# A two-layer diffusion backbone on one core: the start of the first layer reordered around its ada tiles

## The reference

```python
mod_x = (jax.nn.silu(c) @ w_ada[i] + b_ada[i])[:, None, :]
mod_c = (jax.nn.silu(c_ctx) @ w_ada[i] + b_ada[i])[None, None, :]
sh1, sc1, gt1, sh2, sc2, gt2 = jnp.split(mod_x, 6, axis=-1)
csh1, csc1, cgt1, csh2, csc2, cgt2 = jnp.split(mod_c, 6, axis=-1)
hx = rmsnorm(x, g_pre1[i]) * (1.0 + sc1) + sh1
hc = rmsnorm(e, g_pre1[i]) * (1.0 + csc1) + csh1
ux = hx @ w_in[i]
```

## Time and profile before

| | us |
|---|---|
| median of 3 runs (lowest, highest) | 2218.12 (2217.26, 2218.92) |
| time of the profiled execution | 2219.41 |
| span of the profiled execution | 2217.6 |
| TensorE busy in it | 2129.1 (96%) |
| VectorE, ScalarE, POOL busy | 1340.1 (60%), 793.2 (36%), 784.1 (35%) |
| mean granted TensorE clock, share of full | 0.985 |

### The profile page before, as it was taken

How to read it: one execution, slowest core, us unless ns; L and a number is a source line. 1 busy time by engine, 2 the same in 40 slices (tenths; PEclk the granted TensorE clock), 3 DMA queues, 4 the chain that set the end, 5 groups by cost and what they waited for, 6 DMA issues and landing times.

```text
span 2217.6 us, 27943 instructions
## 1 busy us (share of the span) xinstructions
PE 2129.1 (96%) x11302; PEld 1805.5 (81%) x11302; DVE 1340.1 (60%) x1814; ACT 793.2 (36%) x1152; POOL 784.1 (35%) x359
## 2 busy tenths in 40 slices
PE   6999999999999999999999989899999999999997
PEld 6877788888888888888888877778777877888885
DVE  6469899855874687847616665889854352101113
ACT  2447612233324523222212345662244353222223
POOL 3320023232335433323323346103444465444442
PEclk9999999999999999999999989999999999999998
DMA  7110011132344143533323222002222332233321
GB/s 298 48 38 1 15 53 58 42 120 86 124 149 141 65 127 130 190 100 128 112 79 113 92 90 93 30 1 80 84 84 90 122 97 87 94 95 95 95 86 67
DMA packets 63200, 205.24 MB, mean 93 GB/s; under 512 B 7136, under 2 KB 8288, under 8 KB 62816
## 3 DMA queue, kind: packets, MB, share of 16 engines
q1 hardware_dynamic: 57744, 190.87, 26.7%
q10 hardware_dynamic: 5328, 12.59, 1.5%
HBM read 197.79 MB, written 5.64 MB: 92 GB/s over the span
## 4 chain that ended last, share of the span: by engine, by line
PE 78%; DVE 16%; ACT 2%; DMA 1%; issue 1%; POOL 1%; ACTq 0%; DVEq 0%; SPq 0%
PE ps L534 71%; DVE conv_acc L1644 3%; DVE ps L1644 2%; DVE unit_stats L1605 2%; PE ps L560 2%; DVE pt0l L1625 1%; DVE pt1l L1625 1%; DVE probs L1619 1%; PE ps L597 1%; PE ps L744 1%; PE ps L578 1%; DMA w_raw<-in_w 1%; PE ps L618 1%; PE ps L588 1%; POOL w_l L430 1%
## 5 line engine op out<-in xcount | busy, mean ns | idle before, releaser
L430 POOL TENSOR_TENSOR w_l<-w_raw,w_h 128x1024 fp32r<-128x1024 f32 (+3 forms) x296 | 684.5, 2317 | 1280.6 <-ACT w_h L901 1280.4
L534 PE MATMUL ps<-h_h,w_h 128*128 128x512 f32 (+1 forms) x1296 | 427.9, 370 | 8.2 <-ACT t L1159 4.2
L534 PE MATMUL ps<-h_l,w_h 128*128 128x512 f32 (+1 forms) x1296 | 425.0, 368 | 0.0
L534 PE MATMUL ps<-h_h,w_l 128*128 128x512 f32 (+1 forms) x1296 | 424.6, 368 | 0.0
L901 ACT ACTIVATE w_h<-w_raw 128x1024 fp32r<-128x1024 f32 (+3 forms) x296 | 280.5, 950 | 227.4 <-PE ps L534 148.8
L534 PEld LDWEIGHTS ps<-h_h,w_h 128*128 128x128 f32 x1296 | 243.6, 189 | 58.4 <-ACT t L1159 6.6
L534 PEld LDWEIGHTS ps<-h_h,w_l 128*128 128x128 f32 x1296 | 244.7, 189 | 43.4
L534 PEld LDWEIGHTS ps<-h_l,w_h 128*128 128x128 f32 x1296 | 244.2, 188 | 42.1 <-issue 1.2
L1499 DVE CUSTOM_DVE_ANT_0 ps<-ada_raw,c_row 128x1024 f32<-128x1024 f32 x160 | 268.0, 1675 | 9.5 <-DMA ada_raw<-in_ada 4.5
L534 PE MATMUL ps<-f_h,w_h 128*128 128x258 f32 (+1 forms) x672 | 173.1, 339 | 0.9 <-DVE t L1830 0.9
L534 PE MATMUL ps<-f_h,w_l 128*128 128x258 f32 (+1 forms) x672 | 173.5, 340 | 0.0
(11 more groups left out here) (244 smaller groups left out, 3224.3 us busy)
## 6 DMA issues: line engine op xcount, KB each, us to landing
w_raw<-in_w SPq DMA_DIRECT2D x222, 512.0 KB, 3.6
ada_raw<-in_ada SPq DMA_DIRECT2D x80, 512.0 KB, 3.7
w_raw<-in_w SPq DMA_DIRECT2D x50, 256.0 KB, 3.2
ada_first<-in_ada SPq DMA_DIRECT2D x16, 512.0 KB, 6.6
w_raw<-in_w SPq DMA_DIRECT2D x16, 384.0 KB, 3.1
x<-in_x ACTq DMA_DIRECT2D x8, 384.0 KB, 17.5
x_again<-in_x ACTq DMA_DIRECT2D x8, 384.0 KB, 8.7
x_between<-x SPq DMA_DIRECT2D x8, 384.0 KB, 2.3
```

What stands on the lines that cost most here:

```text
L430: nc.gpsimd.tensor_tensor(wl[:, s % RING, 0:n], raw[:, s % RAW, 0:n], wh[:, s % RING, 0:n], ALU.subtract).then_inc(split, 1)
L534: ins = nc.tensor.matmul(at(out, c0, c1), w[:, s % RING, b * P:(b + 1) * P], m[:, kt, first + c0:first + c1], start=(kt == 0 and n == 0), ...
```

## The change

- x is loaded first: tiles 0 to 3 at the head of SP's queue, 4 to 7 on ScalarE's; of const only the first 256 columns come early, the tables (cos, sin and others) behind the ada tiles. c_row is no longer loaded: TensorE spreads silu(c) over the partitions into PSUM (`spread_c`), and VectorE copies it into c_row for the later tiles.
- The first dots read silu(c) from PSUM (`c_spread`) and write their products to SBUF.
- Each x square is summed by itself (eight sums); VectorE squares tiles 1 and 3, ScalarE the others. POOL adds nothing.
- The token factors are copied to SBUF (t1) and multiplied into x by VectorE tile by tile (`by_token_factor`). Each tile's gain is made right behind its two dots (`scale_tile`).
- ScalarE makes each h tile in one step from x, gain and shift (`first_high`), once rounded as the high part and once unrounded, from which POOL subtracts; POOL makes all eight low parts.
- Ada tiles 0 and 1 are made on TensorE before the pair, tiles 2 to 7 inside it (`first_pair`). Each waits for ScalarE's shift of the tile before.
- The value tile's context part lies in the unused quarter of the key's region. In layer 0 its copy waits for the key's eviction, and q0 waits for that copy, as the second of two pieces.
- Slabs 0 to 3 of both layers are loaded, rounded and split with 4 blocks instead of 8. There are twelve places for the first ada tiles.

The diff's new parts come in the order SP, POOL, TensorE, ScalarE, VectorE.

```diff
-ADA_SLOTS = 6
+ADA_SLOTS = 12
...
 def slab_blocks(s):
+    if s < S_Q:
+        return 4
...
-        pool_lows, pool_last, pool_adds = (1, 3, 5), (0, 2, 4, 6), (4, 6)
...
+        pool_last, pool_adds, dve_squares = (0, 2, 4, 6), (4, 6), (1, 3)
...
+        def c_spread(s):
+            return psf[:, 2048 + D * s:2048 + D * (s + 1)]
+        def shift_sums(k):
+            return psf[:, 2 * k:2 * k + 2]
+        def value_piece(ly, c0, c1):
+            return psf[:, 1024 + c0:1024 + c1] if ly == 0 and c0 < CTX else at(A[0], c0, c1)
...
-            sp.dma_start(c_row[:], io["c_row"]).then_inc(c_row_loaded, 16)
-            load(0, KT)
-            load(1, KT)
-            for n in range(ADA_START):
-                if n == ADA_START // 2:
-                    load(2, 4)
-                    load(3, 4)
...
+            for k in range(KT // 2):
+                sp.dma_start(x[:, k, :], io["x"][:, k, :]).then_inc(x_loaded[k], 16)
+            load_first(0)
+            load_first(1)
+            load_run(0, 2)
+            for n in range(2, ADA_START):
+                if n == ADA_START // 2:
+                    load_run(2, RING)
+                load_first(n)
+            sp.dma_start(const[:, C_BLK:NC], io["const"][:, C_BLK:NC]).then_inc(tables_loaded, 16)
...
             split_run(0, 2)
-            for k in range(1, KT, 2):
-                add_squares(0, "pre1", 0, k)
+            lows(0, "pre1", 0, range(2))
             split_run(2, RING)
-            lows(0, "pre1", 0)
+            lows(0, "pre1", 0, range(2, KT))
...
+            def first_pair(s):
+                steps = []
+                for k in range(KT):
+                    steps += [("high", k)] + ([("low", k - 1)] if k else [])
+                steps.append(("low", KT - 1))
+                for i, (kind, k) in enumerate(steps):
...
+                        pe.wait_ge(*seen("hh", 0, "pre1", k))
+                    else:
+                        pe.wait_ge(*seen("hl", 0, "pre1", k))
...
+                    n = {("high", 0): 2}.get((kind, k), k + 3 if kind == "low" else KT)
+                    if n < KT:
+                        shift_tile(n)
...
+            def spread_c():
+                for s in range(2):
+                    for b in range(KT):
+                        ins = nc.tensor.matmul(c_spread(s)[:, b * P:(b + 1) * P],
+                                               silu_c[:, b, s:s + 1].to_broadcast([P, P]), ident, start=True, stop=True)
+                ins.then_inc(*pe_done.up("c_spread"))
             def shift_tile(k):
                 n = 2 * k
+                if k:
+                    pe.wait_ge(*seen("shift", k - 1))
...
-            for k in range(0, KT, 2):
-                shift_tile(k)
-                shift_tile(k + 1)
-                square_sum(0, "pre1", 0, k)
-            pe.wait_ge(*seen("free", "ada", 0, 0))
+            for k in range(KT):
+                if k == 3:
+                    pe.wait_ge(*seen("silu"))
+                    spread_c()
+                square_sum(k)
+            last_use["B"] = last_use["OD"] = ("c_spread",)
+            spread(0, "pre1", 0, "pre1", w=1, to=at(A[1], 0, T))
+            shift_tile(0)
+            shift_tile(1)
...
+            def first_high():
+                act.wait_ge(*seen("spread", 0, "pre1"))
+                nc.scalar.activation(t1[:, 0:T], at(A[1], 0, T), ACT.Copy).then_inc(
+                    *act_out.up("free", "spread", 0, "pre1"))
+                rounds(1)
+                def shift(k):
+                    act.wait_ge(*seen("ada", k))
+                    nc.scalar.activation(mod[:, 0, k, :], shift_sums(k), ACT.Identity,
+                                         bias=vec[:, 0, V_BADA + k:V_BADA + k + 1]).then_inc(*act_tmp.up("shift", k))
+                def modulated(out, k, tally, *name):
+                    for c0, c1, s in chunks(0):
+                        ins = nc.scalar.activation(out[:, c0:c1], x[:, k, c0:c1], ACT.Identity,
+                                                   scale=gain[:, 0, 0, k, s:s + 1], bias=mod[:, 0, k, s:s + 1])
+                    ins.then_inc(*tally.up(*name))
+                shift(0)
+                for k in range(KT):
+                    act.wait_ge(*seen("shift", k))
+                    act.wait_ge(*seen("gain", k))
+                    act.wait_ge(*seen("xn", k))
+                    modulated(hh[:, k], k, act_hi, "hh", 0, "pre1", k)
+                    if k + 1 < KT:
+                        shift(k + 1)
+                    modulated(scaled_tile(k), k, act_tmp, "t", 0, "pre1", k)
+                    if k == 1:
+                        rounds(RING - 1)
...
+            def scale_tile(k):
+                n = 2 * k + 1
+                dve.wait_ge(ada_first_loaded[n % ADA_SLOTS], 16 * (n // ADA_SLOTS + 1))
+                ada_dots(ADA_PE + k, first_slot(n), ada_raw[:, 0, :], c_spread)
...
+            def by_token_factor(k):
+                dve.wait_ge(*seen("free", "spread", 0, "pre1"))
+                v.tensor_tensor(x[:, k, :], x[:, k, :], t1[:, 0:T], ALU.mult).then_inc(*dve_out.up("xn", k))
+            for k in range(KT):
+                scale_tile(k)
+                for n in ((0, 1), (2,), (3,), (4,), (5,), (6,), (7,), ())[k]:
+                    by_token_factor(n)
...
                 dve.wait_ge(used, s0 + S_KV + 4)
-                v.tensor_copy(tile_rows["v"][0][:, 0:T], at(A[0], 0, T)).then_inc(*dve_out.up("free", "gemm", ly, "v"))
+                if ly == 0:
+                    dve.wait_ge(tables_loaded, 16)
+                for c0, c1, s in reversed(chunks(0)):
+                    if ly == 0 and s:
+                        dve.wait_ge(*seen("free", "gemm", ly, "k"))
+                    v.tensor_copy(tile_rows["v"][0][:, c0:c1], value_piece(ly, c0, c1)).then_inc(
+                        *(dve_out.up("free", "gemm", ly, "v") if s else dve_out.up()))
```

More of the change, by code:

```diff
@@ L215, in build @@
         gain = sb("gain", [LAYERS, 4, KT, 2])
+        scale_b = sb("scale_b", [KT])
         ust = sb("unit_stats", [4, 16])
@@ L571, in keep_warm @@
                     nc.tensor.matmul(psf[:, 512:1024], wh[:, s % RING, 0:P], wh[:, s % RING, 0:512], start=True, stop=True)
+            def first_pair(s):
[4 more added lines that the diff above has]
+                for i, (kind, k) in enumerate(steps):
+                    sa = s + 2 * (k // 4)
+                    b = k % 4
+                    if kind == "high":
+                        if b == 0:
+                            pe.wait_ge(split, sa + 2)
+                        pe.wait_ge(*seen("hh", 0, "pre1", k))
+                    else:
+                        pe.wait_ge(*seen("hl", 0, "pre1", k))
+                    first, last = i == 0, i == len(steps) - 1
+                    for n, (w, m) in enumerate(((wh, hh), (wl, hh)) if kind == "high" else ((wh, hl),)):
+                        for c0, c1, ctx_part in chunks(0):
+                            ins = nc.tensor.matmul(at(A[1], c0, c1), w[:, sa % RING, b * P:(b + 1) * P], m[:, k, c0:c1],
+                                                   start=first and n == 0, stop=last and not ctx_part)
+                    if kind == "low" and b == 3:
+                        ins.then_inc(used, 1)
+                    for n, (w, m) in enumerate(((wh, hh), (wl, hh)) if kind == "high" else ((wh, hl),)):
+                        for c0, c1, ctx_part in chunks(0):
+                            ins = nc.tensor.matmul(value_piece(0, c0, c1), w[:, (sa + 1) % RING, b * P:(b + 1) * P],
+                                                   m[:, k, c0:c1], start=first and n == 0 and not ctx_part, stop=last)
+                    if kind == "low" and b == 3:
+                        ins.then_inc(used, 1)
+                    n = {("high", 0): 2}.get((kind, k), k + 3 if kind == "low" else KT)
+                    if n < KT:
+                        shift_tile(n)
@@ L991, in _ @@
             act.dma_start(vec[:], io["vec"]).then_inc(const_loaded, 16)
-            act.dma_start(const[:], io["const"]).then_inc(const_loaded, 16)
-            for k in range(KT):
+            act.dma_start(const[:, 0:C_BLK], io["const"][:, 0:C_BLK]).then_inc(const_loaded, 16)
+            for k in range(KT // 2, KT):
                 act.dma_start(x[:, k, :], io["x"][:, k, :]).then_inc(x_loaded[k], 16)
@@ L996, in _ @@
             nc.scalar.activation(silu_c[:], cvec[:], ACT.Tanh, scale=0.5).then_inc(*act_tmp.up("ctanh"))
[L998 to L1001 removed]
+            table_for(ACT.Sqrt)
+            squares_in()
             for ly in range(LAYERS):
@@ L1493, in modulation, with ada_dots @@
                 dve.wait_ge(*dve_tmp.ago())
-            def ada_dots(k, tile, scratch):
+            def ada_dots(k, tile, scratch, rows):
                 for s in range(2):
-                    link(v.tensor_tensor_reduce(out=scratch, in0=tile, in1=c_row[:, s, :], scale=1.0, scalar=0.0,
```

(14 more changed lines are left out.)

156 lines of the change are left out of this document (55 added, 101 removed).

## The result

| | before | changed |
|---|---|---|
| median of 7 executions, us | 2218.17 (2215.86 to 2222.88) | 2235.23 (2219.06 to 2240.05) |
| profiled execution, us | 2219.41 | 2226.6 |
| its span, mean granted clock | 2217.6, 0.985 | 2224.8, 0.979 |

The ratio of the means (2231.7 and 2218.8 us) is 1.0058, 95% interval 1.0037 to 1.0079: slower by 8 to 18 us. The forecast was 2224.0, between 2216 and 2232. The sign held and the profiled execution is near where the sum put it. The mean, however, lies at the upper end of the range, and the median of the seven above it. The executions of the changed kernel differ by 21 us, those of the kernel before by 7.

The account below looks back on a forecast made before the run. TensorE, busy 96% of the span and at the lower clock in the start, was taken to bound the kernel. q0 3.2 us later plus 2.6 for the clock made +5.8: 2218.1 to 2223.9, rounded 2224.0; range 2216 to 2232.

Parts of the forecast that it names:

- pair starts: TensorE's pair of products in the start: to begin at 44.2 us, 16.6 us before the 60.80 of the kernel before.
- clock low in the pair: TensorE in the pair: 8 us at the lower clock, costing 4 us; called the widest term.
- ada tile 7 done: TensorE finishes the last ada tile inside the pair at 71.1 us; ends of the term 66.1 and 86.9.
- last gain: VectorE's dots, gains and x products beside the pair: last gain at 65.9 us, covered by TensorE; each gain 0.15 us.
- slab 4 split: POOL's low part of slab 4, behind the last h tile's: done at 78.1 us, against 76.8 before.
- from there to q0: Slab 6's load, its rounding, the key's square and scaled copy, the value's context copy: 6.7 us, q0 at 84.8.
- slow steps at q0: Idleness of some 8 us before q0 lowers TensorE's clock for its first products: +2.6 us, bounds 0 and 3.5.
- new tail: Operations from ada tile 7 through slab 4, slab 6, key and value copy to q0: q0 3.2 us later than before.
- Rival 5: TensorE's clock stays low through the pair: ada tile 7 at 86.9, q0 at 100.6, time 2239.7 us; chance 0.07.
- Rival 6: VectorE's dots are slowed by POOL all the same, 2.65 us each: last gain at 86, 2238.4 us; chance 0.05.
- Rival 3: Small products at full clock too: pair starts at 29.5, VectorE then bounds, -11.6 us, 2206.5 us; chance 0.08.
- Costed at nothing: Layer-border half slabs, layer 1's value copy in two pieces, const's late tables, c_row's removed work: no cost counted.

Follow-up runs that it names:

- a_again: The changed kernel once more, unaltered: 2227.17 us, ratio 1.0042 to the kernel before; its profiled execution took 2222.85 us.
- a_third: The changed kernel unaltered, run again for one more profile: 2233.16 us.
- e_q0free: The changed kernel with q0 waiting only for the value tile's latent piece, not the context piece: 2216.32 us, ratio 1.0012 to the kernel before.
- e_evict: The changed kernel with layer 0's key evicted before ScalarE rounds slab 6: 2223.88 us, ratio 1.0015 to the kernel before.
- b_vwait: The kernel before, with only its copy of the value tile made to wait for the key's eviction: 2221.81 us, ratio 1.0015.
- e_wide_tiles: The changed kernel with its eight ada tiles on TensorE made 128 columns wide: 2222.47 us, ratio 1.0018 to the kernel before.
- e_warm: e_wide_tiles plus 34 dense products with unused results in the idle time before q0: 2220.01 us, ratio 1.0011 to the kernel before.
- e_wide_free: The changed kernel with token sums and ada tiles 128 columns wide, q0 waiting for the value's latent piece alone: 2212.87 us, ratio 0.9969 to the kernel before.
- e_wide: The changed kernel with its ada tiles and eight token sums 128 columns wide: 2218.42 us, ratio 1.0001 to the kernel before.

## Why the prediction was right or wrong

| step | predicted | profile | |
|---|---|---|---|
| first token sum | 9.5 | 10.33 | right |
| silu(c) spread done | 24.1 | 24.2 | right, the clock rose within it |
| last sum done | 33.3 | 34.7 | right |
| pair starts | 44.2 | 45.29 | right |
| clock low in the pair | 8 us | 45.3 to 54 | right here, not in half of the executions |
| ada tile 7 done | 71.1 | 71.89 | right here |
| last gain | 65.9 | 67.8 | gains 0.3 to 0.8 us, not 0.15 |
| slab 4 split | 78.1 | 80.2 | one operation missed |
| from there to q0 | 6.7 | 6.7 | right |
| q0 | 84.8 | 86.89 | 2.1 late |
| slow steps at q0 | 2.6 | 2.0 | right, on a wrong ground |

**The sum.** +5.8 us was forecast and +7.2 came in the profiled execution; over all seven it was +12.9 by the means. That the first profile lay so near the sum is in part luck: in a_again's the pair started 5 us earlier and ada tile 7 was done at 66.72, in a_third's it was done at 79.42. The forecast's mechanism, an earlier start that the interleaved tiles and the longer tail give back, held in all three profiles. The tail's part of it is shown by e_q0free and e_evict from one side (q0 6.4 and 5.5 us earlier with the wait gone or cut short) and by b_vwait from the other (the wait alone costs 1 to 6 us). What the tiles do to the clock is shown by e_wide_tiles.

**The new tail was 1.3 us short.** q0 came 2.1 us later than forecast; 0.8 of it was there at ada tile 7. For the tail I listed shift, high part, modulated tile and low part of tile 7. On ScalarE the modulated tile 6 stands between the shift of tile 7 and its high part, 1.2 us, as the changed text has it (the shift of k + 1 comes before the second form of k). With slab 4 that late, each later link held: 3.57 us for slab 6, its rounding, the two evictions, the copy.

**The clock in the pair was given the wrong chances.** The term that was mis-sized, at 8 us at the lower level, rests on "I stay near the lower end because the earlier trace rows shows a rise after 5.2 us". It measured 8.7 and 9 us in the first two profiles and 25 in a_third's. The steps of the earlier trace rows were dense products alone. In the changed pair products of two columns lie between, and the clock of the same program rose near 54 us in one execution and near 70 in another. Rival 5, low through the whole pair, had 0.07; no profile reached its 86.9 for ada tile 7 (a_third 79.42), but half of the executions, 2233 to 2240, lie between the forecast's own range and that rival's 2239.7 or just above, and they put the median of the seven at 2235. The range should have reached to about 2240. That the earlier trace rows and the sums of the earlier trace rows bounded the clock at both ends was right; to take a point between them as a fixed duration was not. e_wide_tiles is the evidence: with the tiles 128 columns wide the long group is gone.

**The slow steps at q0** cost 2.0 us against 2.6, but the 2.6 was taken from a stretch that doesn't show it. The pair of the kernel before was slow from its start, and the earlier trace rows has the spread of 55.23, ahead of its 2.6 us of idleness, at the lower level already; that idle time did not bring the clock down. b_vwait (3.6 us idle, eight slow steps) and e_warm are the evidence for the term.

**Dots and x products.** The dots took 1.21 us each, at most 1.22, with silu(c) in PSUM, also beside POOL; before they took up to 3.26. This line of the changed kernel shows duration in ns, min/median/max:

```profile
L1544 DVE CUSTOM_DVE_ANT_0 ada_raw<-ada_near,ps x10: 1208/1215/1221, 35.2 to 66.0; 128x1024 f32<-128x1024 f32 x10
...
L1590 DVE TENSOR_TENSOR x<-x,t x8: 944/948/2021, 39.2 to 63.8; 128x768 f32<-128x768 f32 x8
```

Rival 6 is out. The x products were held once (2.02). What I had not seen is the gain: costed at 0.15, it took 0.29 alone and, when held, up to 0.82 here and 1.76 in e_wide_free. The Trainium skill's "SBUF — State Buffer", section "Who interferes with whom", counts `tensor_scalar` among the operations that can contend with POOL for the port they share, if its operands meet certain conditions. The gain is a `tensor_scalar`, and the trace agrees: it ends with POOL's low part, at 37.59 and 37.57 us in e_wide_free.

**Rival 3 (all at full clock)** failed as the earlier trace rows said: the last five sums took 0.174 us an instruction on the mean. e_wide made it true by other means, pair at 34.23, and then, as that rival had it, VectorE bound.

**Costed at nothing** held: at the layer border TensorE waited 5.8 us for ScalarE's high parts against 5.9.

## What to carry to other kernels

Read what a moved wait stands behind, not how long it is: a copy of 0.4 us put q0 behind a rounding, a load and an eviction, and cost 6 us and the clock. Small products between dense ones can keep TensorE at half speed and make the time of one program vary by 20 us; where a product's time hardly depends on its columns, making it wide costs almost nothing. Here that gained 3 to 7 us in the kernel before, while the change as it was made lost 8 to 18. A small VectorE operation can take five times its own time beside a GpSimd one; look at when each is issued. Time several executions before believing one profile, and compare the mean granted clock of the short and the long ones.

## What was not expected of the hardware

The width of a float32 product hardly counts between 2 and 128 columns. At the lower level an ada tile of 16 instructions took 3.41 us with two columns and 3.51 with 128 (e_wide_tiles), at full speed 1.84 and 1.95: 3% and 6% more. And one program in two executions, with the same instructions and gaps, reached full speed 16 us apart.
